# Causal attention beside projection matmuls: score matmuls gathered into fewer visits on TensorE

## What is computed

```python
for layer in range(DEPTH):                       # DEPTH = 2
    h = rmsnorm(x, attn_norm[layer])
    if layer % 2 == 0:                           # 16 heads in two groups
        qa, ka, va, qb, kb, vb, qi, ki, wi = split_cols(h @ w_in_even[j], sizes_even)
        o_a = moba_attention(qa, ka, va, table_a)                 # heads 0-7, causal
        o_b = dsa_attention(qb, kb, vb, qi, rmsnorm(ki, ...), wi, table_b)
    else:
        qc, kc, vc = split_cols(h @ w_in_odd[j], sizes_odd)
        o_c = dilated_mixture(qc, kc, vc, table_c)                # 16 heads, causal
    x = x + mixed @ w_o[layer]
    x = x + conv_ffn(rmsnorm(x, ffn_norm[layer]), ...)
```

## Time and profile before

| | before |
|---|---|
| median of 3 runs | 2355.82 us (2355.58 to 2356.02) |
| the profiled execution, its time | 2352.5 us |
| its span in the profile | 2350.7 us |
| busy PE, DVE, ACT, POOL | 2319.3, 1426.2, 1089.3, 408.6 us |
| granted TensorE clock, mean | 0.998 of full speed |
| layer 0 (attention) | about 20 to 340 us of the span |
| layer 1 (attention) | about 693 to 948 us |

### The profile page before, as it was taken

One profiled execution on the slowest core, in us unless ns is written; L12 is line 12 of the kernel. 1 busy time (PEld: TensorE's weight loads), 2 busy tenths in 40 slices (PEclk: granted clock), 3 DMA queues, 4 the chain that ended last, 5 costly groups with the idle time before them and its releaser, 6 DMA issues.

```text
span 2350.7 us, 30161 instructions
## 1 busy us (share of the span) xinstructions
PE 2319.3 (99%) x11870; PEld 1864.1 (79%) x11870; DVE 1426.2 (61%) x2280; ACT 1089.3 (46%) x1772; POOL 408.6 (17%) x304
## 2 busy tenths in 40 slices
PE   9999999999999999999999999999999999999998
PEld 7567678888887777888888878778887889888887
DVE  5887568858654546674676475557777335543443
ACT  4455654424435445442444356675555324432442
POOL 0001322202210001221122130012222222220222
PEclk9999999999999999999999999999999999999999
DMA  5122143433423223444342221011111432232231
GB/s 178 65 88 77 54 157 130 153 121 126 146 88 108 72 68 94 171 157 133 104 159 101 91 88 70 11 48 55 54 50 45 135 119 84 99 110 88 99 110 61
DMA packets 69933, 233.03 MB, mean 99 GB/s; under 512 B 8000, under 2 KB 10176, under 8 KB 69536
## 3 DMA queue, kind: packets, MB, share of 16 engines
q1 hardware_dynamic: 69792, 231.11, 29.4%
HBM read 224.18 MB, written 4.28 MB: 97 GB/s over the span
## 4 chain that ended last, share of the span: by engine, by line
PE 63%; DVE 5%; ACT 2%; issue 1%; DMA 0%; POOL 0%; DVEq 0%; SPq 0%; ACTq 0%
PE psum L478 17%; PE psum L480 17%; PE psum L479 17%; PE psum L1097 1%; PE psum L1122 1%; PE psum L1141 1%; PE psum L2011 1%; PE psum L2012 1%; PE psum L2013 1%; PE psum L1272 1%; PE psum L1283 1%; PE psum L1295 1%; DVE wL L465 1%; DVE ssum L2745 1%; DVE X L2716 0%
## 5 line engine op out<-in xcount | busy, mean ns | idle before, releaser
L478 PE MATMUL psum<-hH,wH 128*128 128x512 f32 (+1 forms) x1904 | 764.2, 401 | 5.6 <-DVE hL L632 2.7
L480 PE MATMUL psum<-hH,wL 128*128 128x512 f32 (+1 forms) x1904 | 740.7, 389 | 0.0
L479 PE MATMUL psum<-hL,wH 128*128 128x512 f32 (+1 forms) x1904 | 739.2, 388 | 0.0
L465 DVE TENSOR_TENSOR wL<-raw,wH 128x1024 fp32r<-128x1024 f32 (+2 forms) x353 | 447.4, 1268 | 357.8 <-ACT wH L460 355.8
L460 ACT ACTIVATE wH<-raw 128x1024 fp32r<-128x1024 f32 (+2 forms) x353 | 363.3, 1030 | 480.5 <-PE psum L480 479.3
L478 PEld LDWEIGHTS psum<-hH,wH 128*128 128x128 f32 x1904 | 358.1, 188 | 108.5 <-issue 37.6
L480 PEld LDWEIGHTS psum<-hH,wL 128*128 128x128 f32 x1904 | 357.8, 188 | 74.7
L479 PEld LDWEIGHTS psum<-hL,wH 128*128 128x128 f32 x1904 | 358.6, 188 | 62.3 <-issue 0.7
L1845 POOL TENSOR_TENSOR sg<-sg,cv 128x512 f32<-128x512 f32 x66 | 95.1, 1441 | 677.2 <-ACT sg L1674 677.2
L478 PE MATMUL psum<-gH,wH 128*128 128x512 f32 x506 | 197.5, 390 | 0.0
L480 PE MATMUL psum<-gH,wL 128*128 128x512 f32 x506 | 196.8, 389 | 0.0
(11 more groups left out here) (379 smaller groups left out, 3362.6 us busy)
## 6 DMA issues: line engine op xcount, KB each, us to landing
raw<-in_up SPq DMA_DIRECT2D x132, 512.0 KB, 3.6
raw<-in_dn SPq DMA_DIRECT2D x48, 704.0 KB, 4.0
raw<-in_win SPq DMA_DIRECT2D x56, 512.0 KB, 3.6
mbuf<-in_wmod SPq DMA_DIRECT2D x48, 512.0 KB, 3.7
raw<-in_we SPq DMA_DIRECT2D x33, 512.0 KB, 3.7
raw<-in_wq SPq DMA_DIRECT2D x24, 512.0 KB, 3.6
tm<-toep SPq DMA_DIRECT2D x32, 256.0 KB, 4.2
raw<-in_wo SPq DMA_DIRECT2D x32, 256.0 KB, 2.6
```

Of the source, the lines that this page charges most:

```text
L465: ve.do.tensor_tensor(flat_of(wLb, n), flat_of(rawb, n), flat_of(wHb, n).bitcast(F), ALU.subtract).then_inc(*w_lo.up(n))
L478: pe.do.matmul(o, H[:, k, :], high(k), start=k == 0, stop=False)
L479: pe.do.matmul(o, H[:, k, :], low(k), start=False, stop=False)
L480: ins = pe.do.matmul(o, L[:, k, :], high(k), start=False, stop=k == kt - 1)
```

## The change

1. **Scores in two visits.** The four query blocks of a pair are taken in the order 3, 1, 2, 0 (`block_of`). PE scores blocks 3 and 1 together at step 4p, blocks 2 and 0 together at step 4p+1. Block 1 goes to banks 6 and 5, block 0 to the upper columns of banks 0 and 1. The products with v use bank 7 alone.
2. **New waits of PE.** The visit at step 4p waits for the `PT` copy of step 4p-2 (`at_c`), since block 1's scores enter bank 5; the transposes of step 4p (block 3, banks 4 and 5) wait until DVE has reduced block 1's scores (`at_m` of step 4p+1).
3. **Index scores two at a time**, into three bank pairs (4, 6, 0), begun at tick 54, between the index query units; the order of the items is changed so that the last query unit is not needed early.
4. **The list** gives the first ten steps of layer 0 seven ticks, the next fourteen six, then six of four and four of three; the keeps begin at item 11 and go 2, 3, 2, 3 a pair of steps.
5. `turn` of v comes after two ticks instead of four where a `wo` unit follows. POOL's masked adds follow the new block order.

```diff
-            out_ = [("ticks", 72)]
+            out_ = [("ticks", 54)]
             for n in range(24):
-                out_ += [("ticks", 1), ("index", n), ("ticks", 1)] + ([("keep", 1)] if n >= 8 else [])
-            per = [(3, 3)] * 24 + [(2, 1)] * 10 + [(0, 0)]
+                out_ += [("ticks", 1)] + ([("scores", n)] if n % 2 == 0 else [])
+                out_ += [("index", n), ("ticks", 1)] + ([("keep", 1)] if n >= 11 else [])
+            out_.append(("ticks", 2))
+            per = [(4, 3)] * 10 + [(3, 3)] * 14 + [(2, 2)] * 6 + [(2, 1)] * 4 + [(0, 0)]
...
-            keep = [("keep", 3 if s % 4 == 0 else 2)] if a.layer == 0 and s < 16 else []
+            keep = [("keep", 2 + s % 2)] if a.layer == 0 and s < 16 else []
...
+            elif what == "scores" and scores is not None:
+                for i in range(n, n + 2):
+                    scores(i)
...
-                if i == 3 and before_.kind == "v":
+                if i == (1 if x.kind == "wo" else 3) and before_.kind == "v":
                     turn(before_)
...
+    index_items = [(1, c) for c in range(7)] + [(2, 0), (2, 1), (2, 2), (1, 7)] + [(2, c) for c in range(3, 8)]
+    index_items += [(3, c) for c in range(8)]
...
+    def index_bank(n):
+        return (4, 6, 0)[n % 3]
...
-        if n >= 2:
-            pe.wait_ge(*sc_rl.at(n - 2))
+        if n >= 3:
+            pe.wait_ge(*sc_rl.at(n - 3))
...
+        def block_of(self, s):
+            return (3, 1, 2, 0)[s % 4]
+
+        def score_at(self, s, u):
+            i = self.block_of(s)
+            if i == 1:
+                return bank[(6, 5)[u]][:, :256]
+            return bank[u][:, 384:512] if i == 0 else bank[u][:, :128 * (i + 1)]
...
-            if s < 32:
-                p, i = s // 4, s % 4
-                W = 128 * (i + 1)
+            if s < 32 and s % 4 < 2:
+                p = s // 4
+                these = (s, s + 1) if s % 4 == 0 else (s + 1, s + 2)
...
+                if s and s % 4 == 0:
+                    pe.wait_ge(*at_c.at((a.key, s - 2)))
...
-                for u in range(2):
-                    r0 = 64 * u
-                    ins = pe.do.matmul(bank[u][:, :W], qT[r0:r0 + 64, p % 3, i * 128:i * 128 + 128],
-                                       kT[r0:r0 + 64, p % 3, :W], start=True, stop=True)
-                ins.then_inc(*at_s.up((a.key, s)))
+                for q in these:
+                    i = a.block_of(q)
+                    for u in range(2):
+                        r0 = 64 * u
+                        ins = pe.do.matmul(a.score_at(q, u), qT[r0:r0 + 64, p % 3, i * 128:i * 128 + 128],
+                                           kT[r0:r0 + 64, p % 3, :128 * (i + 1)], start=True, stop=True)
+                    if q == these[0]:
+                        ins.then_inc(*at_s.up((a.key, q)))
+                ins.then_inc(*at_s.up((a.key, these[1])))
...
+                if q % 4 == 0:
+                    pe.wait_ge(*at_m.at((a.key, q + 1, 1)))
```

More of the change, by code:

```diff
@@ L772, in layer_order, with follow @@
         else:
-            out_ = [("ticks", 72)]
+            out_ = [("ticks", 54)]
             for n in range(24):
-                out_ += [("ticks", 1), ("index", n), ("ticks", 1)] + ([("keep", 1)] if n >= 8 else [])
-            per = [(3, 3)] * 24 + [(2, 1)] * 10 + [(0, 0)]
+                out_ += [("ticks", 1)] + ([("scores", n)] if n % 2 == 0 else [])
+                out_ += [("index", n), ("ticks", 1)] + ([("keep", 1)] if n >= 11 else [])
+            out_.append(("ticks", 2))
+            per = [(4, 3)] * 10 + [(3, 3)] * 14 + [(2, 2)] * 6 + [(2, 1)] * 4 + [(0, 0)]
             last = 2 + 32
         for s, (n, m) in enumerate(per):
-            keep = [("keep", 3 if s % 4 == 0 else 2)] if a.layer == 0 and s < 16 else []
+            keep = [("keep", 2 + s % 2)] if a.layer == 0 and s < 16 else []
             out_ += [("half", s), ("ticks", n), ("half", s)] + keep + [("ticks", m)]
         return out_ + [("ticks", last)]
-    def follow(a, ticks, steps, index=None, keep=None):
+    def follow(a, ticks, steps, index=None, keep=None, scores=None):
         for what, n in layer_order(a):
@@ L902, in ve_fill @@
                 if x.c >= 3:
-                    ve.wait_ge(*at_s.at((attn[layer].key, 4 * (x.c - 3) + 3)))
+                    ve.wait_ge(*at_s.at((attn[layer].key, 4 * (x.c - 3) + 2)))
                 elif layer and x.u == 0:
@@ L1249, in __init__, with turns_of @@
             self.key, self.layer, self.n = key, layer, 32
+        def block_of(self, s):
[5 more added lines that the diff above has]
+            return bank[u][:, 384:512] if i == 0 else bank[u][:, :128 * (i + 1)]
+        def turns_of(self, s):
+            n = self.block_of(s) + 1
+            return (bank[4][:, :256] if n == 1 else ps[2]).rearrange("p (u b n) -> p u b n", u=2, n=128)[:, :, 0:n, :]
         def end_of(self, s):
@@ L1282, in pe_pairs @@
                         c0 = 64 * u
-                        ins = pe.do.matmul(bank[6 + p % 2][c0:c0 + 64, 128 * b:], vR[:, p % 3, b, c0:c0 + 64],
+                        ins = pe.do.matmul(bank[7][c0:c0 + 64, 128 * b:], vR[:, p % 3, b, c0:c0 + 64],
                                            PT[:, u, b, 128 * b:], start=b == 0, stop=b == 3)
@@ L1336, in ve_pairs @@
                 ve.wait_ge(*at_fh.at((a.key, p)))
-                ve.do.tensor_tensor(in_blocks(mixL[:, p, :]), turned(bank[6 + p % 2]), in_blocks(mixH[:, p, :]).bitcast(F),
+                ve.do.tensor_tensor(in_blocks(mixL[:, p, :]), turned(bank[7]), in_blocks(mixH[:, p, :]).bitcast(F),
                                     ALU.subtract).then_inc(*at_low.up((a.key, p)))
             if s < 32:
-                p, i = s // 4, s % 4
+                p, i = s // 4, a.block_of(s)
                 W = 128 * (i + 1)
@@ L1368, in is_masked @@
     def is_masked(a, s):
-        return a.key == "E0" and s >= 16 and s % 4 > 0
+        return a.key == "E0" and s >= 16 and a.block_of(s) > 0
     def sp_toeplitz(sp, a, p):
@@ L2945, in tensor_program @@
         ins.then_inc(*warm_p.up(0))
-        follow(E0, pe_fill(pe, 0), pe_pairs(pe, E0), lambda n: pe_index(pe, n))
+        follow(E0, pe_fill(pe, 0), pe_pairs(pe, E0), scores=lambda n: pe_index(pe, n))
         pe_ffn(pe, 0)
```

51 lines of the change are left out of this document (28 added, 23 removed).

## The result

The changed kernel takes **2335.6 us** (median of 4 runs, 2334.55 to 2338.82). The kernel before, run beside it, takes 2355.74 (2355.58 to 2356.02). The ratio is 0.9922, with a 95% interval of 0.991 to 0.9934: faster by 0.8%, some 18 us by the ratio. The forecast was 2339 in a range of 2334.5 to 2347.

The account below looks back on a forecast made before the run. PE's own instruction stream was taken to set the time. Terms -18.0 - 1.9 + 3.0 = -16.9 took the profiled 2352.5 us to 2335.6; with before's median 3.3 above its profile, the forecast was 2339 us, range 2334.5 to 2347.

Parts of the forecast that it names:

- Visits: Scores and index scores in both layers: 44 fewer PE visits at a fixed 0.41 us each, -18.0 us.
- the choice between 0.41 and 0.30: Saving per merged visit: 0.41 us if the second block is free, 0.30 if its weight load is exposed (13.2 in all).
- Waits at layer 0's end: PE's waits for `vR` (1.2 us), `PT` (0.5) and before the first step (0.2) go: -1.9 us, bounds 0 and -2.
- DVE's lag and the bias rows: Layer 0's first pair: PE waits about 2.5 us, then 0.5 to 1 at the transposes; +3.0 us, bounds 0 and 6.
- The terms at zero: Possible costs put at 0, among them DVE in layer 0's steps, the masked step 16 and the wait for `PT`.
- DVE in steps 0 to 15: Layer 0's pairs: DVE, 23.4 us against PE's 27.3 a pair at first, works off its lag in two pairs; cost 0.
- Step 16: Masked block 3 needs POOL's adds, 3.02 us, covered because keeps end some 4 us before; cost 0, uncovered up to 3.
- The wait for `PT` before the merged visit: The copy takes under 1 us, three ticks (2.1 us) before the visit, 1.4 in layer 0's last pair; cost 0.
- Rival 1: Score visits: each change of block exposes a weight load of 0.11 us, gain shrinks by 4.8, 2344 us; chance 0.08.
- Rival 2: Layer 0: DVE becomes the bound, PE waits some 3 us a pair, 12 in all, 2351 us; chance 0.08.
- Rival 3: All 16 pairs: transposes wait for block 1's reduction, 1.6 us a pair, 26 in all, slower at 2365 us; chance 0.03.
- Rival 4: Visits: the 0.41 us is stream catch-up time, given back between gathered visits, so no change, 2356 us; chance 0.03.

Follow-up runs that it names:

- turn_late: The changed kernel with v turned four ticks into the wo unit, as before the change; 2337.46 us, ratio 0.9928.
- tm_early: The changed kernel with the bias rows of pairs 0 and 1 loaded 32 ticks earlier; 2334.09 us, ratio 0.9917.
- best: tm_early with one keep instead of two at layer 0's first step; 2333.03 us, ratio 0.9911.
- old_list: The changed kernel's gathered visits with the list of the kernel before; 2340.13 us, ratio 0.9942.
- probe_half: The changed kernel with 16 extra visits in layer 1, each one unused 128-wide float32 matmul on 64 rows; 2346.61 us, ratio 0.9969.
- probe_full: The changed kernel with 16 extra visits in layer 1, each one unused 128-wide float32 matmul on all 128 rows; 2340.31 us, ratio 0.9942.
- index_only: The kernel before, its list otherwise unchanged, with index scores two items a visit and three bank pairs; 2352.28 us, ratio 0.999.

## Why the prediction was right

**Visits, -18.0.** Right in mechanism and size. Every column stayed and 44 fixed prices went. The starts gave 0.41 a visit; layer 1 measured 0.427, so that the term is 18.8. Of the missing 0.02 a third is the base: undisturbed projection matmuls start 0.227 apart (687.27 to 689.99 us before, twelve intervals), not 0.23. The rest lies behind a visit: the intervals after the first two are up to 0.235 for a while, outside the three starts from which I took the price. The prediction said nothing of why a visit has a fixed price; the probes and the products with v show that it goes with using a part of the array. Reading the price as an intercept from two widths was sound; the six-matmul visit of window attention was the right witness that a second block pays nothing. It fixed the choice between 0.41 and 0.30, and the 2.14 and layer 1 confirmed it.

**Waits at layer 0's end, -1.9.** All three are gone; by the starts they were 2.4, so the term was 0.5 too small. The reason given for `vR` was most of the truth: turn_late has 1.1 of 1.5 back.

**DVE's lag and the bias rows, +3.0.** The waits are at the two places named, and 1.87 + 1.43 = 3.3 long, against 2.5 and "0.5 to 1". The mechanism holds: DVE stood waiting for `tm` just before the first, and tm_early took it away. DVE's own lag was forecast at 5.2 us behind PE's first visit and would have been 4.6 (PE's visit at 96.9, DVE free at 101.5). tm_early shows that the rows made 2.3 of the 3.3; best, that one keep too many made the other 1.0.

**The terms at zero.** DVE in steps 0 to 15: right, old_list has waits at the first pair alone. Step 16: right for PE, but not for the reason given. The keeps were to end some 4 us ahead; in the trace the mask is made at 202.52 us, POOL begins its adds at 203.08, and DVE waits 1.0 and 0.5 us for them, behind PE's visit at 202.61:

```profile
204.51 0.69 DVE L1392 CUSTOM_DVE_ANT_0 Sp<-psum,sq 128x512 f32<-128x512 f32 x1 [0.97 <-POOL sq L1464]
```

PE did not need the result soon, so the zero held by slack. The wait for `PT` before the merged visit was given 0, and was wrong by a little: it costs 0.4, and not in the last pair, where I looked, but at step 16, where ACT makes the copy for step 14 only behind the exponentials of step 15, and those waited 1.94 us for DVE:

```profile
201.88 0.39 PE L480 MATMUL psum<-hH,wL 128*128 128x512 f32 x1
202.61 1.13 PE L1313 MATMUL psum<-kT,qT 64*128 64x512 f32 x4 [0.34 <-ACT PT L1367]
```

**The sum.** -18.8 - 2.4 + 3.7 = -17.5 by the measured terms, -17.9 measured in the profiles, -16.9 forecast; most of the last 0.4 lies in the program's start. The errors of the terms (0.8 and 0.5 too little gained, 0.7 too little lost) partly cancelled, which was luck. The median came out 3 us below the forecast, and only 1.1 above the lower end of the range, chiefly because I carried over that before's median lay 3.3 above its profiled execution: the changed kernel's lies 1.1 above its profile. By the profiles such an offset is one of scattered half-clock stretches, which another kernel's runs need not share; for the runs without a profile this is not shown. In the later groups before's median is 2353.9.

**The rivals.** Rival 1 (the load shows) fell by 2.14 against 2.27. Rival 2 (DVE as the bound) fell by old_list, in which DVE has less time still in the first ten steps. Rival 3 (a wait at all 16 pairs) fell: layer 1 has no new wait and layer 0 one pair with any. Rival 4 (the 0.41 is time in which the stream catches up) fell by layer 1's 6.83, and by probe_half, where visits put back cost their full price.

## What to carry to other kernels

Where the engine that sets the time switches between kinds of work, take the price of a switch from starts at two widths (the intercept), look in the trace for a place where two blocks already share one visit, and multiply by the visits that can be merged. Then go to the first consumer behind the shortened stretch: whatever fed it just in time (here bias rows issued behind a weight tick, and top-k rounds queued ahead of its reduction) is now late, and two small moves there were worth another 3 us on top of the 17.

## What was not expected of the hardware

- The fixed 0.4 us belongs to matmuls on a part of the array between matmuls on all of it: a 128-wide probe visit cost 0.64 us on 64 rows and 0.26 on 128, and the products with v, on all rows but 64 columns, have some 0.35 beyond what they stream. Work on the whole array slips in at its columns' price. Transposes do so too: the changed kernel's two at 129.22 us take 0.68 from the matmul before to the second behind, less 0.46 is 0.22, as in probe_full. What the array does in that time isn't settled.
- Gathering by three gave back practically all of its 1.7 us: 1.3 at the first pair, 0.3 at an index visit.
- Waits of PE of 2 us or so were in some executions followed by a stretch at the lower clock level (index_only's 0.72 above) and in others not: the changed kernel waits 1.8 and 1.3 us and keeps a clock of 1.00 from 103 to 112 us. One such stretch costs some 1.7 us, more than several of the terms that were forecast.
